# One decoder layer on one core: gate products moved one tile ahead in the token mixers, and the merge's first loads issued in the mixers' last stretch

## The reference

```
h = rmsnorm(x, g) * (1 + sc1) + sh1
proj = h @ w_in          # q, f, i, g | b, c, v | mga (1024 cols), mgb (1024 cols)
ya, state = hgrn2_branch(q, f, i, g, s0)       # gated linear recurrence, 4 heads
yb, state = short_conv_branch(b, c, v, buf0)
mixed = sigmoid(mga) * (ya @ w_out_hgrn) + sigmoid(mgb) * (yb @ w_out_conv)
x = x + g1 * (mixed @ w_o)
# then routing to 64 experts, top 8, a shared expert, the final norm
```

## Time and profile before

| what | us |
|---|---|
| median of 3 executions (2238.17 to 2243.89) | 2240.93 |
| the profiled execution, its own time | 2239.09 |
| its span, first to last instruction | 2237.5 |
| PE busy | 1983.2 (89%) |
| DVE busy | 1037.5 (46%) |
| ACT busy | 889.0 (40%) |
| POOL busy | 345.6 (15%) |
| mean granted TensorE clock, share of full | 0.953 |

### The profile page before, as it was taken

One profiled execution on the slowest core, in us unless ns is written; L12 is line 12 of the kernel. 1 busy time (PEld: TensorE's weight loads), 2 busy tenths in 40 slices (PEclk: granted clock), 3 DMA queues, 4 the chain that ended last, 5 costly groups with the idle time before them and its releaser, 6 DMA issues. The chain is left out here.

```text
span 2237.5 us, 32930 instructions
## 1 busy us (share of the span) xinstructions
PE 1983.2 (89%) x9599; PEld 1472.3 (66%) x9601; DVE 1037.5 (46%) x1508; ACT 889.0 (40%) x1213; POOL 345.6 (15%) x321
## 2 busy tenths in 40 slices
PE   4799999599989799797987999999999999999970
PEld 3799999466656466585544767666666676776750
DVE  3210111534326533453534656556565566666656
ACT  4111110244301221221125666666555666666552
POOL 0100000100000000000111222222222322222220
PEclk9899999799989999898988999999999999999995
DMA  6211110011132177333317999999999789879846
GB/s 228 67 47 39 57 43 13 27 49 41 45 110 75 59 262 252 140 133 118 140 67 307 303 311 298 339 344 342 376 337 375 248 272 290 260 238 304 280 100 246
DMA packets 152434, 424.08 MB, mean 190 GB/s; under 512 B 11455, under 2 KB 76211, under 8 KB 127810
## 3 DMA queue, kind: packets, MB, share of 16 engines
q1 hardware_dynamic: 118258, 298.98, 35.5%
q0 software_dynamic: 31488, 114.93, 19.9%
q10 hardware_dynamic: 2640, 9.54, 1.1%
HBM read 345.93 MB, written 77.49 MB: 189 GB/s over the span
## 5 line engine op out<-in xcount | busy, mean ns | idle before, releaser
L1894 DVE TENSOR_TENSOR wexp_lo<-wexp,wexp_hi 128x2048 fp32r<-128x2048 f32 x190 | 426.8, 2288 | 45.3 <-ACT wexp_hi L1846 41.4
L1846 ACT ACTIVATE wexp_hi<-wexp 128x2048 fp32r x190 | 352.7, 1904 | 52.0 <-issue 49.1
L1827 PE MATMUL bank<-wexp_down,hTe 128*128 x736 | 330.6, 592 | 0.0
L1802 PE MATMUL bank<-wexp_hi,x_hi 128*128 128x512 f32 x744 | 300.1, 403 | 3.8 <-DVE wexp_lo L1894 3.8
L1802 PE MATMUL bank<-wexp_hi,x_lo 128*128 128x512 f32 x744 | 291.9, 392 | 0.0
L1802 PE MATMUL bank<-wexp_lo,x_hi 128*128 128x512 f32 x744 | 290.7, 391 | 0.0
L1776 POOL DMA_INDIRECT acc_d<-ob,ixs x92 | 158.3, 1721 | 655.5 <-DVE ixs L1906 297.6
L540 PE MATMUL bank<-hT,wg 128*128 128x344 f32 x768 | 236.1, 461 | 7.5 <-ACT gst L551 7.3
L1827 PEld LDWEIGHTS bank<-wexp_down,hTe 128*128 128x128 f32 x736 | 139.1, 189 | 139.4 <-issue 132.3
L540 PEld LDWEIGHTS bank<-hT,wg 128*128 128x128 f32 x768 | 144.0, 192 | 95.8 <-ACT gst L551 16.7
L442 PE MATMUL bank<-hT_hi,w_hi 128*128 128x344 f32 x576 | 186.9, 324 | 14.8 <-DVE w_lo L509 14.8
(11 more groups left out here) (320 smaller groups left out, 2695.8 us busy)
## 6 DMA issues: line engine op xcount, KB each, us to landing
wexp<-in_w_exp_gate SPq DMA_DIRECT2D x64, 1024.0 KB, 6.6
wexp<-in_w_exp_up SPq DMA_DIRECT2D x64, 1024.0 KB, 10.4
wexp_down<-in_w_exp_down SPq DMA_DIRECT2D x64, 1024.0 KB
wada<-in_w_ada SPq DMA_DIRECT2D x12, 2048.0 KB, 12.0
w_raw<-in_w_in SPq DMA_DIRECT2D x28, 512.0 KB, 3.9
gates_d<-gst POOLq DMA_DIRECT2D x48, 172.0 KB, 2.1
gate<-gates_d SPq DMA_DIRECT2D x16, 516.0 KB, 5.1
wg<-in_w_in SPq DMA_DIRECT2D x16, 512.0 KB, 4.0
```

Source lines behind the costliest of these rows:

```text
L1802: last = pe.matmul(banks[0][:].rearrange("p (g n) -> p g n", g=2), stat[:, b, k, :], mov[:, b, :, k * FF:(k + 1) * FF], start=(k == 0 and ...
L1827: last = pe.matmul(banks[4 + half][:], hT[:, f, :], wdn[:, bass.ds(slot, 1), f, half * 512:half * 512 + 512].rearrange("p a n -> p (a n)") ...
L1846: act.activation(w_hi[:, b, g, :], wexp[:, bass.ds(e & (RING - 1), 1), g, :].rearrange("p a n -> p (a n)"), ACT.Copy).then_inc(whi_ok, 1)
L1894: dve.tensor_tensor(w_lo[:, b, g, :], wexp[:, bass.ds(e & (RING - 1), 1), g, :].rearrange("p a n -> p (a n)"), w_hi[:, b, g, :], ALU.subtr ...
```

## The change

It does three things.

1. **Gate tile 0 goes first.** In the mixers' first block TensorE computes all three products of gate tile 0 before `prepare(0, 0)`, and in group g those of tile g + 1. ACT copies product 0 out before it waits for `f_ok` and starts `prepare(0, 0)`, product 1 in the middle of it, product 2 behind it. The first block now holds 9 gate tiles (27 products) and POOL's loop there stores 9.
2. **The second block starts at tile 9**: 21 products instead of 24. Those behind sample tokens and in norm items stay, so of the 4 by themselves 1 is left.
3. **The merge's first loads move.** `gate` and `wo` get fixed places on top of `fT` and what follows it (`cvT`), both dead by then. SP issues `load_branch` for tiles 0 and 1 (eight transfers) in the mixers' second block, behind its last gate weights, after waits for the stores of gate tiles 0 to 9 and for the first norm item. In the merge SP starts with `wada`. Their semaphores `w_ok` are no longer cleared with a stage.

The two `first` below are ACT's and, with the gate products, TensorE's; the last part is SP's in the merge.

```diff
+                at3 = -(-nc.sbuf_base // 32) * 32
                 fT = sb("fT", [P, CH, TT], ctx=c3)
+                gate_t = [nc.alloc_sbuf_tensor_at(f"gate{j}", [P, 2, TT], F32, offset=at3 + j * 2 * TT * 4) for j in range(2)]
+                wo_t = [nc.alloc_sbuf_tensor_at(f"wo{j}", [P, 2, CH, P], F32, offset=at3 + 4 * TT * 4 + j * 2 * CH * P * 4)
+                        for j in range(2)]
...
+                def load_branch(sp, t, j):
+                    for x in range(2):
+                        sp.dma_start(wo_t[j][:, x], out_w[x][:, :, bass.ds(t * P, P)]).then_inc(w_ok[j], 16)
+                        sp.dma_start(gate_t[j][:, x, :], gates_d[bass.ds(t + x * KD, 1)].rearrange(
+                            "a p t -> p (a t)")).then_inc(w_ok[j], 16)
...
-            prepare(0, 0)
+            first()
...
-                with pool.Fori(0, GROUPS) as g:
+                with pool.Fori(0, GROUPS + 1) as g:
                     store_gate(pool, g)
...
                 act.activation(lbt[:, 0:2, :], lbt[:, 0:2, :], ACT.Exp).then_inc(lb_ok, 1)
+                act.wait_ge(const_ok, 5)
+                take_gate(act, 0, 0)
                 act.wait_ge(f_ok, 1)
-                act.wait_ge(const_ok, 5)
...
-                    ahead(lambda: take_gate(act, g, 0))
-                    take_gate(act, g, 1)
-                    take_gate(act, g, 2)
+                    ahead(lambda: take_gate(act, g + 1, 0))
+                    take_gate(act, g + 1, 1)
+                    take_gate(act, g + 1, 2)
...
+                def first():
+                    prepare(0, 0, lambda: take_gate(act, 0, 1))
+                    take_gate(act, 0, 2)
...
-                    gate_product(pe, g, b, 0)
+                    gate_product(pe, g + 1, 1 - b, 0)
...
+                def first():
+                    for n in range(PIECES):
+                        gate_product(pe, 0, 0, n)
+                    prepare(0, 0)
...
                 for t in range(GROUPS + 2 + NS // PIECES, 2 * GROUPS):
                     next_weights(t)
+                for n in range(PIECES):
+                    sp.wait_ge(gate_out[n], 16 * (KD + 2))
+                sp.wait_ge(ya_ok, 1)
+                for j in range(2):
+                    load_branch(sp, j, j)
                 sp.wait_ge(u_ok, 1)
...
-                gate = iter([(t, n) for t in range(GROUPS, 2 * GROUPS) for n in range(PIECES)])
+                gate = iter([(t, n) for t in range(GROUPS + 1, 2 * GROUPS) for n in range(PIECES)])
-                for _ in range(GROUPS * PIECES - NS - len(norm_items)):
+                for _ in range((GROUPS - 1) * PIECES - NS - len(norm_items)):
...
-                for j in range(2):
-                    load(j, j)
                 for j in range(2):
                     load_ada(j, j)
```

More of the change, by code:

```diff
@@ L361, in layer @@
                 next_stage()
+                w_ok = [top.enter_context(nc.semaphore(f"w_ok{j}")) for j in range(2)]
+                out_w = [a[n].rearrange("l (k p) n -> p (l k) n", p=P) for n in ("w_out_hgrn", "w_out_conv")]
+                def load_branch(sp, t, j):
[3 more added lines that the diff above has]
+                            "a p t -> p (a t)")).then_inc(w_ok[j], 16)
                 token_mixers(nc, a, o, sb, sem, banks, par, ident, eps, w_in, gates_d, hT, qT, fT, gT, bT, cvT, vv,
-                             (O_LB, O_HG, O_CW, O_CB))
+                             (O_LB, O_HG, O_CW, O_CB), load_branch)
             mix = top.enter_context(ExitStack())
@@ L368, in layer @@
             next_stage()
-            merge(nc, a, sb, sem, banks, gates_d, qT, bT, hT_hi, mT_lo, wo_raw, wo_in, condition, ada_v, b_ada_v, mod_v)
+            merge(nc, a, sb, sem, banks, gates_d, qT, bT, hT_hi, mT_lo, wo_raw, wo_in, condition, ada_v, b_ada_v, mod_v,
+                  wo_t, gate_t, w_ok, load_branch)
         next_stage()
@@ L605, in slot, with groups @@
             return (CPG * b + j) % (2 * CPG) if j in (0, CPG) else j
-        def groups(eng, prepare, finish, enter=None, leave=None):
-            prepare(0, 0)
+        def groups(eng, first, prepare, finish, enter=None, leave=None):
+            first()
             with eng.Fori(0, PAIRS - 1) as i:
@@ L673, in finish @@
                                    ACT.Copy).then_inc(v_ok, 1)
-                    ahead(lambda: take_gate(act, g, 0))
-                    take_gate(act, g, 1)
-                    take_gate(act, g, 2)
+                    ahead(lambda: take_gate(act, g + 1, 0))
+                    take_gate(act, g + 1, 1)
+                    take_gate(act, g + 1, 2)
                     act.wait_ge(o_ps, g + 2)
                     act.activation(grp(qT, g), h3(o_b[:]), ACT.Copy).then_inc(o_ok, 1)
-                groups(act, prepare, finish)
+                def first():
+                    prepare(0, 0, lambda: take_gate(act, 0, 1))
+                    take_gate(act, 0, 2)
+                groups(act, first, prepare, finish)
             @block.vector
@@ L741, in finish @@
                             dve.sem_inc(S_ok, 1)
-                groups(dve, prepare, finish, lambda i: s.enter(i, 2 * (3 + CPG * H)), s.leave)
+                groups(dve, lambda: prepare(0, 0), prepare, finish, lambda i: s.enter(i, 2 * (3 + CPG * H)), s.leave)
             @block.tensor
@@ L793, in finish @@
                     last.then_inc(o_ps, 1)
-                groups(pe, prepare, finish)
+                def first():
+                    for n in range(PIECES):
+                        gate_product(pe, 0, 0, n)
+                    prepare(0, 0)
+                groups(pe, first, prepare, finish)
             @block.sync
@@ L873, in _ @@
                                    pattern=[[-1, NS], [0, P]], channel_multiplier=1).then_inc(sel_ok, 1)
-                with pool.Fori(GROUPS, 2 * GROUPS) as t:
+                with pool.Fori(GROUPS + 1, 2 * GROUPS) as t:
                     store_gate(pool, t)
@@ L1002, in load_out, with merge @@
     sp.dma_start(wo_raw[:, c % 2], a["w_o"].rearrange("l (k p) n -> p (l k) n", p=P)[:, 2 * c:2 * c + 2, :]).then_inc(wo_in[c % 2], 16)
-def merge(nc, a, sb, sem, banks, gates_d, yaT, ybT, m_hi, m_lo, wo_raw, wo_in, condition, ada_v, b_ada_v, mod_v):
+def merge(nc, a, sb, sem, banks, gates_d, yaT, ybT, m_hi, m_lo, wo_raw, wo_in, condition, ada_v, b_ada_v, mod_v,
+          wo, gate, w_ok, load):
     with ExitStack() as ctx:
-        wo = [sb(f"wo{j}", [P, 2, CH, P], ctx=ctx) for j in range(2)]
-        gate = [sb(f"gate{j}", [P, 2, TT], ctx=ctx) for j in range(2)]
+        sb("branch_room", [P, 4 * TT + 4 * CH * P], ctx=ctx)
         part = sb("part", [P, 2, 2, PIECE], ctx=ctx)
@@ L1025, in _ @@
             def _(sp):
-                def load(t, j):
-                    for x in range(2):
-                        sp.dma_start(wo[j][:, x], out_w[x][:, :, bass.ds(t * P, P)]).then_inc(w_ok[j], 16)
-                        sp.dma_start(gate[j][:, x, :], gates_d[bass.ds(t + x * KD, 1)].rearrange(
-                            "a p t -> p (a t)")).then_inc(w_ok[j], 16)
                 def load_ada(n, j):
                     sp.dma_start(wada[j][:], ada_v[:, :, bass.ds(n * 512 + FIRST * 512, 512)]).then_inc(ada_in[j], 16)
-                for j in range(2):
-                    load(j, j)
                 for j in range(2):
@@ L1046, in _ @@
                         sp.wait_ge(free, (2 * i - 1 + j) * PIECES + 3)
-                        load(2 * i + j, j)
+                        load(sp, 2 * i + j, j)
                         sp.wait_ge(mod_ps, 2 * i - 1 + j)
```

9 lines of the change are left out of this document (4 added, 5 removed).

## The result

The changed kernel takes 2218.62 us (median of 4, 2216.73 to 2222.2); the kernel before, measured beside it, 2240.03 (4, 2238.17 to 2243.89). The ratio is 0.9901 with an interval of 0.9888 to 0.9913: 21.4 us less, where 17.5 was forecast. Over all executions of the study the unchanged kernel has a median of 2238.60 (58) and the changed one of 2219.55 (14): 19.0 less. Between the profiled executions it is 2239.09 - 2220.11 = 19.0.

A forecast was written before the change was run, and what follows sets the result against it. TensorE was taken to bound the group loop, second block and most of the merge, idling in the mixers' and merge's openings. 16.4 + 7.2 - 6.1 = 17.5 us took the median from 2240.93 to 2223.4, range 2218 to 2231.

The forecast's parts named there:

- Part 1: Mixers' second block: three standalone gate products leave it, 16.4 us gained.
- What was named as late next: Second block: first norm item's reciprocal, held 1 us by DVE's convolution until 695.53, absorbed in the second item.
- Part 2: Mixers' opening: the three products enter it, first starting at 414.0 when its weights land; 6.1 us lost.
- Part 3: Merge's opening: loads issued in the mixers let TensorE start when the engines are ready; 7.2 us gained.
- the forecast's 1.15 us: Merge's opening: DVE's first output comes 1.15 us behind the landing of `badd` (802.58 to 803.73).
- The first: Mixers' opening: POOL's addition waits for its memsets, start 417.7, loss 9.8 instead of 6.1 us, 2227.1; chance 0.2.
- The second: Merge's opening: DVE's wait for `badd` decides, gain 4.6 us (2226.0) or nothing (2230.6); chance 0.12.
- The fourth: Mixers' opening: products fill no idle time, opening grows at most 18.4 us, 2235.7; chance 0.04.
- The third, the low clock: Mixers' opening: TensorE stays at 1.2 GHz into the groups, 2256 if low to group 0's end; chance 0.02.
- "All later stages only move": Stages behind the edited places: shifted in time only, adding nothing to the sum of 17.5 us.

The follow-up runs named there:

- The order alone: Changed kernel with the merge's first loads issued in the merge as before, only the gate products reordered; 2229.5 us (0.9947), run again 2229.07 (0.9953).
- with the wait put in: Changed kernel with POOL waiting for the end of its memsets before its addition to `gate_read`; 2221.62 us (0.9924).
- the loads alone: Changed kernel with every gate product back in its old place, only the merge's first loads moved; 2230.72 us (0.9968).
- `badd` first: Changed kernel with the four `badd` transfers ahead of the two of `wada` in the merge; 2222.21 us (0.9927).
- the repeats: Changed kernel run twice more without an edit, beside the kernel before; 2217.47 us (0.9906) and 2221.8 us (0.9916).
- the kernel that split DVE's sums: Changed kernel with gate tile 0's weights loaded in the input projection, and two of DVE's eight `hT` sums given to POOL; 2220.9 us (0.992).

## Where the prediction was right, and the steps of it that failed

**Part 1, the second block.** Forecast 16.4 us less, measured 16.17. What was named as late next is: DVE enters the first norm item right behind the convolution, at 700.31 where 702 was expected, and TensorE's rhythm doesn't feel it.

The order alone has the same short second block (134.16 and 133.29).

**Part 2, the opening.** The start was forecast 4.16 us behind the block's (the weights' landing), measured 4.17. Its length at the low clock was forecast as 7.05, measured 6.58; the copies leave 0.60 and 0.55 as forecast. The attention was forecast at 21.85 behind, measured 21.52. The transposes of group 1, forecast 6.1 us later than before, are 5.78 later. The loss at the loop's end is 6.18, and 5.97 at the second block's start, because the handover was 0.21 us shorter. That the sum comes within 0.2 us of the forecast is in part luck: the handover alone took 2.27 to 2.88 us in three profiles of the changed kernel. The Trainium skill says that an engine's sequencer pushes engine instructions into a queue and executes control instructions itself (Perfetto Trace Analysis, Sequencer Loop). The trace agrees: the start is at 4.17 and, with the wait put in, at 7.96. The Trainium skill's price for a change of function set, 2.66 us (ScalarE: Activation LUTs, What ACT_TABLE_LOAD costs), is not what the trace shows: a load began at 419.70 and the next ACTIVATE at 420.99, 1.29 us later, and ACT was waiting for TensorE at 424.66.

**Part 3, the merge.** Forecast 7.2, measured 7.19 in the whole kernel and 7.11 alone. TensorE starts 0.37 us behind SP, where "within 0.3" was named. `badd` was bounded between 10.7 and 19.7 us behind the start and called harmless up to about 17; DVE's first product came at 15.78. The fourth output was ready to run behind the condition at 784.82, and DVE's sum, with its addition to `free` right behind it in the code, started at 783.19. With the forecast's 1.15 us the addition came at 783.4 at the latest, so the margin was about 1.5 us. The 1.15 was read from a row in which TensorE waited for nothing: 803.74 is TensorE's own time, 1.89 us behind its condition as in every tile. So it was an upper bound, and on the safe side. The choice of 7.2 was right, but not by much: the bounds of the forecast reached from harmless to 2.6 us, and only the run could tell. Moving the wait to 7.38 changed nothing.

**The rivals.** The first was built, and the opening is 3.8 to 3.9 us longer by it; it is absent from the changed kernel. The second is refuted by the 15.78, by the loads alone and by `badd` first. The fourth is refuted by the opening, where only 5.97 of 18.4 us were paid. The third, the low clock, was priced for the wrong place: the first product does bring TensorE up, as forecast, but the clock can fall later, in the loop, in some executions. It cost some 0.7 us in the changed kernel (the output matmuls of group 0 took 3.95 us instead of 3.66, and the group behind them 24.46 instead of 24.05) and 7 us in one execution of the kernel with the order alone.

**The steps that failed.** The three terms sum to 17.5 forecast and, with 0.26 of the barrier, 17.65 measured. The measured median nevertheless came out 4.8 us under the forecast of 2223.4, and the gain was 21.4 us instead of 17.5. Two steps of the sum failed.

1. **From the profiled execution to the median.** The prediction took the profiled execution of before to lie 1.8 us under the median and added 1.8 us. That was the scatter of a median of three. Over 58 executions the median is 2238.60, 0.5 us below that profile, not 1.8 above it; and the changed kernel's profile lies 1.5 us above the median of its four (0.6 above that of all 14). The mis-sized term accounts for 1.8 + 1.5 = 3.3 of the 4.8 us.
2. **"All later stages only move".** The stages that nobody edited were put at nothing, those ahead of the mixers too. The mixers start 1.47 us earlier, which is the rest of the 4.8 (2220.11 against 2221.6). In the other two profiles of the changed kernel they start 0.8 and 1.1 us earlier than before, so this is not one execution's chance. Its cause stays open.

The same steps explain the gain: 21.4 is 17.65 from the places, 1.47 from the start less 0.1 behind the merge, and 0.9 + 1.5 us by which the two profiled executions lie off the medians beside them, on opposite sides. The last two are chance, and so is the size of the 21.4: the repeats gave 21.1 and 18.3. The measured 2218.62 lies at the very low end of a range, 2218 to 2231, that was stretched upward for two rivals and downward for hardly anything.

## What to carry to other kernels

Idle time at the opening of a stage can be filled with independent work, and the price is not that work's length but what it pushes past the point at which the old first instruction could have started: three products of 16 us cost 6. Read which wait ends last in each place, and ask at once which is next and how far away it is; here the next wait was 1.5 us away in the merge and none at all in the second block, and the forecasts of the places held because each was worked out in its own place. Don't correct a profile's time to a median of three executions whose spread is larger than the correction, and leave room in the range for a microsecond or two from stages that aren't edited.

## What the runs showed of the hardware

**The clock fell while TensorE was busy.** In ten of the eleven profiles of kernels with the opening products one stretch of the low clock follows 42 to 50 us behind the block's start, at the 32-column output matmuls of group 0. The changed kernel's windows and rows:

```profile
452.00:454.00 2.00, 2.00 (x18) 2.00 (x18) 0.00 (x0) 0.00 (x0) 0.00 (x0) 0.89 0.70 233
454.00:456.00 2.00, 2.00 (x8) 1.65 (x8) 0.00 (x0) 1.57 (x3) 0.00 (x0) 0.50 0.00 0
456.00:458.00 2.00, 2.00 (x7) 1.24 (x6) 0.00 (x0) 1.93 (x4) 0.00 (x0) 0.76 0.00 0
```

```profile
450.33 3.95 PE L812 MATMUL bank<-qin,S 128*128 128x32 f32 x32
454.09 1.09 PE L786 MATMUL bank<-ident,kend 128*128 128x128 f32 x4
454.98 5.77 PE L556 MATMUL bank<-hT,wg 128*128 128x344 f32 x16
```

TensorE is busy for all 6 us and the granted clock is 0.50 of full, its level of 1.2 GHz, in the middle one. Transposes take 1.09 instead of 0.64 us and a product 5.77 instead of 4.8. In one execution of the order alone it came back in five later groups. The eleventh profile, of the kernel that split DVE's sums, keeps the full clock at group 0 and has two such stretches, behind groups 1 and 2 (0.55 at 480 to 482 us, 0.52 at 504 to 506). The three profiles without the opening products, two of the kernel before and one of the loads alone, have none in the loop once the clock is up, though they run the same matmuls. Each stretch begins during or right behind a group's 32 matmuls of 32 columns; that these bring it about was not tried, and what the opening products have to do with it stays open.

**DVE's sums slow down beside POOL's.** Sums of 128 x 1032 floats took DVE 1.83 us each on average (10.95 / 6) with POOL's two, 2.83 us each, running beside them for about half of that time, and 1.15 alone.

**The time between blocks scatters.** Between the mixers' two blocks 0.42 to 3.30 us pass, from the end of ACT's last copy to SP's first issue, with 0.42 and 2.33 in two executions of one program.
